# Second block of a two-block transformer kernel: convolution taps spread from attention into retention and short convolution, weight sums issued after the second fold, and one product of an output pair issued early

## The reference, cut to what matters

```python
def conformer_conv(glu_in, w, bias, ln_w, ln_b):
    a, g = jnp.split(glu_in, 2, axis=-1)
    u = depthwise_conv(a * jax.nn.sigmoid(g), w) + bias      # 31 taps
    return jax.nn.silu(layer_norm(u, ln_w, ln_b)).astype(glu_in.dtype)
...
def mixer_output(p, ret_o, att_o, ...):
    r = (head_group_norm(ret_o, ret_gn_w) * jax.nn.silu(p['ret_z'])).astype(dt)
    s = short_conv(p['sc_b'], p['sc_c'], p['sc_x'], sc_conv_w) * jax.nn.silu(p['sc_z'])
    f = conformer_conv(p['cf_glu'], cf_conv_w, ...) * jax.nn.silu(p['cf_z'])
    a = att_o * jax.nn.silu(p['att_z'])
    merged = sum(jax.nn.sigmoid(g) * (br @ w_branch[i])
                 for i, (g, br) in enumerate(zip(gates, (r, s, f, a))))
    return merged @ w_out
...
for l in range(DEPTH):                                       # DEPTH = 2
    px = split_proj(modulate_2(rmsnorm_2(x, norm_w[l]), shift_x, scale_x) @ w_in[l])
    ...                                                      # retention and windowed attention
    x = x + gate_x[:, None] * mixer_output(px, ret_x, att_x, ...)
```

## Time and profile before

| | us |
|---|---|
| median of 3 runs | 3319.2 |
| lowest and highest | 3311.17, 3322.95 |
| profiled execution, its own time | 3317.98 |
| its span | 3316.2 |
| PE busy in the span | 3163.6 |
| DVE busy | 1798.5 |
| ACT busy | 882.0 |

### The profile page before, as it was taken

How to read it: one execution, slowest core, us unless ns; L and a number is a source line. 1 busy time by engine, 2 the same in 40 slices (tenths; PEclk the granted TensorE clock), 3 DMA queues, 4 the chain that set the end, 5 groups by cost and what they waited for, 6 DMA issues and landing times.

```text
span 3316.2 us, 38135 instructions
## 1 busy us (share of the span) xinstructions
PE 3163.6 (95%) x13916; PEld 2101.8 (63%) x13916; DVE 1798.5 (54%) x3620; ACT 882.0 (27%) x1820; POOL 352.4 (11%) x302
## 2 busy tenths in 40 slices
PE   7988998999999999999999999999999999999998
PEld 4743653678853655666665555555557677778887
DVE  2253324788732335886557454444458855754555
ACT  2241221334421222154222221111122622222222
POOL 1300430343300340000120000000000012000000
PEclk9989899999999999999999999999999999999999
DMA  8637786633338796201111112222223011223232
GB/s 271 215 121 251 283 346 204 187 107 102 89 111 270 277 360 195 64 26 45 39 38 51 54 55 57 58 58 57 58 58 83 26 51 51 77 70 89 83 89 64
DMA packets 427399, 397.25 MB, mean 120 GB/s; under 512 B 28080, under 2 KB 362416, under 8 KB 420048
## 3 DMA queue, kind: packets, MB, share of 16 engines
q1 hardware_dynamic: 393520, 352.60, 33.7%
q10 hardware_dynamic: 15264, 22.24, 2.1%
q0 software_dynamic: 18432, 19.98, 1.8%
HBM read 443.54 MB, written 31.92 MB: 143 GB/s over the span
## 4 chain that ended last, share of the span: by engine, by line
PE 60%; DVE 6%; DMA 2%; issue 2%; ACT 2%; ACTq 0%; DVEq 0%
PE psum L768 43%; PE psum L1297 3%; PE psum L994 3%; DVE arena L2315 2%; DMA ring<-in_w_branch 1%; PE psum L1013 1%; PE psum L753 1%; PE psum L1381 1%; PE psum L1421 1%; DVE arena L2312 1%; ACT scratch L1708 1%; PE psum L979 1%; DVE ring L2312 1%; PE psum L1411 1%; PE psum L861 0%
## 5 line engine op out<-in xcount | busy, mean ns | idle before, releaser
L768 PE MATMUL psum<-arena,ring 128*128 128x256 f32 (+1 forms) x2976 | 843.4, 434 | 19.9 <-DVE arena L2312 11.2
L768 PEld LDWEIGHTS psum<-arena,ring 128*128 128x128 f32 x2976 | 562.5, 190 | 269.7 <-DVE arena L2312 15.2
L768 PE MATMUL psum<-hT,ring 128*128 128x256 f32 (+1 forms) x2464 | 696.9, 436 | 0.0
L768 PEld LDWEIGHTS psum<-hT,ring 128*128 128x128 f32 x2464 | 468.2, 190 | 199.5 <-issue 3.2
L1716 ACT ACTIVATE scratch<-psum 128x256 f32<-128x256 f32 (+1 forms) x447 | 190.8, 427 | 1018.3 <-PE psum L768 860.9
L2312 DVE TENSOR_TENSOR psum<-psum,scratch 128x256 f32<-128x256 f32 (+1 forms) x352 | 167.6, 480 | 379.6 <-PE psum L768 273.2
L2312 DVE TENSOR_TENSOR ring<-ring 128x512 f32<-128x512 f32 (+1 forms) x384 | 257.2, 689 | 184.3 <-PE psum L768 172.2
L1716 ACT ACTIVATE arena<-psum 128x512 f32<-128x512 f32 (+5 forms) x426 | 197.3, 497 | 426.8 <-PE psum L768 128.8
L1708 ACT ACTIVATE arena<-psum,cols 128x256 f32<-128x256 f32 (+2 forms) x291 | 134.1, 485 | 498.0 <-PE psum L994 226.5
L2315 DVE SCALAR_TENSOR_TENSOR arena<-arena,vec 128x783 f32<-128x783 f32 (+1 forms) x256 | 228.8, 894 | 9.1
L2315 DVE SCALAR_TENSOR_TENSOR arena<-arena,psum 128x256 f32<-128x256 f32 (+2 forms) x247 | 99.2, 435 | 198.6 <-ACT arena L1708 198.5
(11 more groups left out here) (290 smaller groups left out, 3751.8 us busy)
## 6 DMA issues: line engine op xcount, KB each, us to landing
ring<-in_w_in SPq DMA_DIRECT2D x177, 512.0 KB, 4.2
arena<-in_moe_w SPq DMA_DIRECT2D x44, 1536.0 KB, 10.9
ring<-in_ada_w SPq DMA_DIRECT2D x96, 512.0 KB, 6.0
ring<-in_w_mod SPq DMA_DIRECT2D x48, 512.0 KB, 5.8
ring<-in_ssm_w_in SPq DMA_DIRECT2D x48, 512.0 KB, 5.5
ring<-in_w_branch SPq DMA_DIRECT2D x64, 256.0 KB, 3.1
hT<-in_moe_w SPq DMA_DIRECT2D x10, 1536.0 KB
ring<-in_moe_w SPq DMA_DIRECT2D x10, 1024.0 KB, 5.9
```

What stands on the lines that cost most here:

```text
L768: mm = nc.tensor.matmul(flat(bank_, nb), lhs[:, k, :], rhs(k), start=(start and k == 0), stop=(k == kd_ - 1), skip_group_check=True)
```

## The change

Four things change, all in the second block.

1. In layer 1 (`cx` false) the taps are dealt out anew: 32 in the first pairs (chunk 0 exactly), 2 in each of rounds 0 to 5 (12), and 84 in pairs 1 to 13: 7 in pair 1, 4 in pairs 2, 4, 6 and 8, 8 in pairs 3, 5, 7 and 9 to 12, and 5 in pair 13. Up to three of a pair's taps are its `late` part, between C22 and C12. The total stays 128. Chunk 1 now outlives attention, so layer 1's buffer for it is put into `cT`, and the wait of the gate part for chunk 1's convolution falls away in layer 1.
2. In every `combine` that has a `mid` and a next pair, in both layers, `w_sums` stands behind C22 instead of ahead of it.
3. In pairs 2h + 2 the `mid` taps stand ahead of `ret_states`, in both layers.
4. In `pair` for pair 50, in both layers, PE takes the weights and a bank of pair 51 and issues pair 51's P1 between P5 of pair 50 and the wait for `mrg` chunks 4 to 7. Pair 51 then starts with its P2. The seven products of each pair stay the same.

```diff
--- before.py
+++ after.py
@@ -485,7 +485,8 @@
...
         mQ = Arena(at=late_at)
-        cu = [cu_first, br_free[:, 4 * CW - 813:4 * CW], mQ.take(813), mQ.take(813)]
+        cu = [[cu_first, br_free[:, 4 * CW - 813:4 * CW], mQ.take(813), mQ.take(813)]]
+        cu.append([cu_first, cT.rearrange("p k n -> p (k n)")[:, 0:813]] + cu[0][2:4])
         pT_window = arena[:, k_raw_at:k_raw_at + 3 * S].rearrange("p (a b) -> p a b", b=S)
@@ -611,8 +612,8 @@
...
-            row = cu[c][:, 15:15 + S].rearrange("p (b h n) -> p h b n", h=2, n=P)[:, h]
-            return [(row, 0, 2)] + ([(cu[c][:, 15 + CO + P * h:15 + CO + P * h + P].unsqueeze(1), 2, 3)] if ctx_here("cf_g", l, c) else [])
+            row = cu[l][c][:, 15:15 + S].rearrange("p (b h n) -> p h b n", h=2, n=P)[:, h]
+            return [(row, 0, 2)] + ([(cu[l][c][:, 15 + CO + P * h:15 + CO + P * h + P].unsqueeze(1), 2, 3)] if ctx_here("cf_g", l, c) else [])
@@ -757,11 +758,17 @@
...
-            def pair(a, b, src, ready=None, between=None):
+            ahead = {}
+
+            def pair(a, b, src, ready=None, between=None, then=None):
...
                 nb = blocks(a)
-                wa, used_a = take(a)
-                wb, used_b = take(b)
+                begun = ahead.pop(a, None)
+                if begun is None:
+                    wa, used_a = take(a)
+                    wb, used_b = take(b)
+                else:
+                    (wa, used_a), (wb, used_b), (x, x_full) = begun
@@ -775,16 +782,21 @@
...
                 s = lambda j: sum_tile(a)[:, kd_ * j:kd_ * j + kd_, :]
-                x, x_full = job(*b, "0")
+                if begun is None:
+                    x, x_full = job(*b, "0")
                 if ready == "m":
...
                         eng.wait_ge(vector_done, pe.at(("mrg", a[1], c)))
-                product(x, wa[:, 0:kd_, :], low(0), True, ("P1", a))
+                if begun is None:
+                    product(x, wa[:, 0:kd_, :], low(0), True, ("P1", a))
                 if ready == "m":
...
                     product(z, s(0), total(0), True, ("P5", a))
+                    a_, b_ = then
+                    ahead[a_] = take(a_), take(b_), job(*b_, "0")
+                    product(ahead[a_][2][0], ahead[a_][0][0][:, 0:kd_, :], low(0), True, ("P1", a_))
                     for c in range(4, 8):
@@ -1542,7 +1554,7 @@
...
                     for j in range(4):
-                        pair(*todo[50 + j], mrg, ready="m" if j == 0 else None)
+                        pair(*todo[50 + j], mrg, ready="m" if j == 0 else None, then=todo[51] if j == 0 else None)
                 if upto > 7:
@@ -2117,7 +2129,7 @@
...
                         eng.wait_ge(tensor_done, ac.at(("full",) + j))
-                        act(cu[0][:, 15 + CO:15 + CO + L], bank(j)[:, 0:L], ACT.Tanh, scale=0.5).then_inc(scalar_done, ac.step([("free",) + j, ("cf_t", 0, 0, "c")]))
+                        act(cu[0][0][:, 15 + CO:15 + CO + L], bank(j)[:, 0:L], ACT.Tanh, scale=0.5).then_inc(scalar_done, ac.step([("free",) + j, ("cf_t", 0, 0, "c")]))
                     for i, (one, two) in enumerate(first_pairs(l)):
@@ -2141,7 +2153,7 @@
...
                             eng.wait_ge(tensor_done, ac.at(("full",) + j))
-                            if (c, tag) == (3, "x0"):
+                            if (l, c, tag) == (0, 3, "x0"):
                                 eng.wait_ge(vector_done, ac.at(("cf_conv", l, 1)))
@@ -2366,7 +2378,7 @@
...
                     mid()
-                if nxt:
+                elif nxt:
                     w_sums(*nxt)
@@ -2374,6 +2386,8 @@
...
                     [("C22", a), ("full",) + jb1 if dst_b is None else name_b + ("1",)]))
+                if mid and nxt:
+                    w_sums(*nxt)
                 if late:
@@ -3044,7 +3058,7 @@
...
                         for o in (0, 15 + S) + ((15 + CO + L,) if cx else ()):
-                            v.memset(cu[c][:, o:o + 15], 0.0).then_inc(vector_done, ve.step([("cu_free", l, c)]))
+                            v.memset(cu[l][c][:, o:o + 15], 0.0).then_inc(vector_done, ve.step([("cu_free", l, c)]))
                     if cx:
@@ -3063,9 +3077,9 @@
...
                             if k == 0:
-                                ts(acc, cu[c][:, 0:w_], cw(0, c)).then_inc(vector_done, ve.step())
+                                ts(acc, cu[l][c][:, 0:w_], cw(0, c)).then_inc(vector_done, ve.step())
                             elif k < 31:
-                                stt(acc, cu[c][:, k:k + w_], cw(k, c), acc, ALU.mult, ALU.add).then_inc(vector_done, ve.step())
+                                stt(acc, cu[l][c][:, k:k + w_], cw(k, c), acc, ALU.mult, ALU.add).then_inc(vector_done, ve.step())
                             else:
@@ -3100,22 +3114,22 @@
...
                         b, free = full("cf_a", 0, 0, "c")
-                        u = cu[0][:, 15 + CO:15 + CO + L]
+                        u = cu[0][0][:, 15 + CO:15 + CO + L]
                         stt(u, u, 1.0, b[:, 0:L], ALU.add, ALU.mult).then_inc(vector_done, ve.step(free))
...
                     combine(*first[1], mid=lambda: taps(3))
-                    taps(4 if cx else 7)
+                    taps(4 if cx else 6)
                     combine(*first[2], mid=lambda: taps(6 if cx else 3), late=lambda: (rotate_q(0), rotate_q(1)))
...
                     combine(*first[3], mid=lambda: taps(3))
-                    taps(4 if cx else 7)
+                    taps(4 if cx else 6)
                     combine(*first[4], mid=lambda: taps(6 if cx else 3), late=lambda: (rotate_q(2), rotate_q(3)))
...
                     taps(3 if cx else 1)
-                    combine(*first[5], mid=lambda: taps(6 if cx else 5), late=lambda: taps(3))
+                    combine(*first[5], mid=lambda: taps(6 if cx else 3), late=lambda: taps(3 if cx else 0))
                     glu(3)
@@ -3165,8 +3179,8 @@
...
                         att_norm(r, n, j)
-                        if tap[0] < 64:
-                            taps(min(64 - tap[0], 3 if cx else 5))
+                        if tap[0] < 64 if cx else r < 6:
+                            taps(min(64 - tap[0], 3) if cx else 2)
                         if r % 3 == 2 if cx else r % 2:
@@ -3287,24 +3301,24 @@
...
                     key_scale()
-                    combine(*todo[1], mid=lambda: taps(5))
+                    combine(*todo[1], mid=lambda: taps(5), late=lambda: taps(0 if cx else 2))
                     for h in range(3):
...
                             ret_norm(h - 1, zi[h - 1])
-                        combine(*todo[2 * h + 2], mid=lambda: (ret_states(h), taps(3)))
+                        combine(*todo[2 * h + 2], mid=lambda: (taps(3), ret_states(h)), late=lambda: taps(0 if cx else 1))
                         zi.append(z_mul("ret_z", l, h + 1, cx, h + 1, -0.5))
-                        combine(*todo[2 * h + 3], mid=lambda: taps(6))
+                        combine(*todo[2 * h + 3], mid=lambda: taps(6 if cx else 5), late=lambda: taps(0 if cx else 3))
                         ret_center(h)
...
                     ret_norm(2, zi[2])
-                    combine(*todo[8], mid=lambda: (ret_states(3), taps(3)))
+                    combine(*todo[8], mid=lambda: (taps(3), ret_states(3)), late=lambda: taps(0 if cx else 1))
                     v.memset(sc_u[:, :, :], 0.0).then_inc(vector_done, ve.step())
                     sc_conv(0)
-                    combine(*todo[9], mid=lambda: taps(6))
+                    combine(*todo[9], mid=lambda: taps(6 if cx else 5), late=lambda: taps(0 if cx else 3))
                     ret_center(3)
@@ -3318,9 +3332,10 @@
...
                     for c in (1, 2, 3):
-                        combine(*todo[8 + 2 * c], mid=(lambda: taps(6)) if c < 3 else None)
+                        combine(*todo[8 + 2 * c], mid=(lambda: taps(6 if cx else 5)) if c < 3 else None, late=(lambda: taps(0 if cx else 3)) if c < 3 else None)
                         sc_conv(c)
-                        combine(*todo[9 + 2 * c], mid=(lambda: taps(min(6, 128 - tap[0]))) if c < 3 else cf_center)
+                        combine(*todo[9 + 2 * c], mid=(lambda: taps(min(6 if cx else 5, 128 - tap[0]))) if c < 3 else cf_center,
+                                late=(lambda: taps(min(0 if cx else 3, 128 - tap[0]))) if c < 3 else None)
                         sc_out(c, sc_z(c))
```

## The result

| | before | after |
|---|---|---|
| median of the runs, us (12 each) | 3318.4 | 3300.5 |
| lowest and highest | 3311.17, 3327.77 | 3295.71, 3310.82 |
| profiled execution, its own time and span | 3317.98, 3316.2 | 3296.91, 3295.1 |
| PE, DVE, ACT busy | 3163.6, 1798.5, 882.0 | 3153.5, 1791.4, 881.4 |

The ratio of the times is 0.995, with a 95% interval of 0.994 to 0.996. The kernel became 18 us faster, where 16 were forecast (3303, within 3296 to 3312).

What follows compares the result with a forecast made beforehand. PE was taken as the bound, busy 3163.6 of 3316.2 us, so only its waits could pay. Terms 7.4 + 3.1 + 2.9 - 3.2 + 4.3 + 1.7 = 16.2 gave 3301.8, stated as 3303; range 3296 to 3312.

Steps and rivals of the forecast that it cites:

- Attention, 7.4 forecast: Layer 1's attention: fewer taps a round shorten PE's waits, gaining 7.4 us, between 5.0 and 8.0.
- The first wait: Ahead of round 0's turn in layer 1's attention: PE's 4.9 us wait shrinks by 2.3 to 2.6.
- The half clock: Round 0's turn in attention: a shorter wait may spare PE's spell at 1.2 GHz, worth 1.25 us.
- the later waits: Later attention rounds: two waits of 2.5 us together and one of 1.7 go, 4.2; 3.8 counted.
- The rival in which ACT and banks hold attention: Layer 1's attention: turns wait for copies, only 2.3 of 7.4 us comes, 3308; chance 0.12.
- Weight sums in layer 0's retention, 3.1 forecast: Last products of pairs 3, 5 and 7: three waits for C22 go, 3.1 us, or 2.0 if held.
- Short convolution, 2.9 net forecast: Layer 1's short convolution: four waits for C22, 3.3 us, go; net 2.9 after pair 9's delay, between 1.5 and 3.3.
- The charge of 0.4 at `ret_center(3)`: Pair 9 of layer 1: `ret_center(3)` waits for three late taps and `w_sums`, ending its chain about 0.4 us later.
- Late taps in layer 1's retention, -3.2 forecast: Heads 0 to 2: `w_sums` stretched beside POOL by 1.07 us each delays PE, losing 3.2, between 0.1 and 3.9.
- One product ahead, 4.3 and 1.7 forecast: Pair 50: pair 51's P1 fills PE's wait, gaining 4.3 us in layer 0 (at least 2.6) and 1.7 in layer 1.
- At nothing: Fewer taps in first pairs, taps ahead of `ret_states` and earlier C22 at pair 18: counted as no gain or loss.
- the half clock that I had kept as a lower bound: Pair 19: longer idle time could halve PE's clock once, 1.3 us lost, counted only in the lower bound.

Runs made afterwards that it cites:

- e5: Changed kernel with weight sums back ahead of C22 in layer 1's pairs 3, 5, 7 and 9; layer 1's retention 2.5 us shorter, median not given.
- the four moves: Changed kernel with sums ahead of C22 in rotations, pairs 3, 5, 7, 9 and pair 18, and round 0's taps behind `att_max(1)`; median 3291.3 us.
- e3: Kernel before the change with only the weight sums moved behind C22; layer 0's retention gains 3.9 us, median not given.
- e6: Changed kernel with POOL scaling only two of four query tiles in layer 1's retention, computation incomplete; median of six runs 3302.56 us.
- e2: Changed kernel with the weight sums ahead of C22 again; median 3300.8 us.
- e4: Changed kernel with weight sums ahead of C22 again in the first pairs with rotations; stretch through layer 1's attention 2.6 us shorter, median not given.

## Why the prediction was right, and where its terms were off

The sum was 16.2. From layer 0's retention on, the trace gained 16.0 (15.5 with layer 0's first pairs and attention); the median gained 17.9. That is closer than the terms were.

**Attention, 7.4 forecast.** The dealing alone gives 9.2 to 10.2 in part D (against the two executions with the old dealing). The first wait shrank by 2.6 rather than 2.3. The kernel with five taps in round 0 gives 2.36 for three taps. The other 0.3 is that the first of round 0's taps is now the first of chunk 1, a `tensor_scalar` of 0.49, where each of the five before was one of 0.78. The half clock went as forecast, 1.5 by start times, but in part by luck: behind the same 2.30 it fell in one of six executions (e5). All 4.2 of the later waits went, and each wait also takes the overlap of its neighbours with it, 0.2 to 0.3, which no row of waits shows. The rival in which ACT and banks hold attention did not come with two taps a round; at the first turn ACT did become the last to be waited for with the four moves, once round 0's queue on DVE was 1.6 shorter still.

**Weight sums in layer 0's retention, 3.1 forecast, 3.9 measured** (A, twice). The waits shown were three, 3.1; the 0.8 above it is 0.27 for each, the same overlap.

**Short convolution, 2.9 net forecast.** The four waits went, as forecast; with the overlaps they were worth 4.4 (E and F of e3). Their cause was half right: the sums' place alone clears them, and five taps in place of six, which alone clear 2.2 of 3.3, add nothing beside it. The charge of 0.4 at `ret_center(3)` was 1.0, and 1.6 more for a half clock that no term held.

**Late taps in layer 1's retention, -3.2 forecast, -1.5 measured.** The step that failed is the size: I took the excess of the earlier trace rows, 1.07, on each head in full, and named waits of about 1.4 a head, where 0.82 came. In the changed kernel the sums overlap only the second of POOL's instructions and take 2.71, an excess of 0.69, and the idle time ahead of `ret_center` swallowed 0.2 of it. The prices fit each other: 1.77 us of idle time without late taps (e3), less 2.33 of taps, leaves `ret_center` 0.56 late; 0.50 was measured; with sums at 2.01 (e6) nothing is left. The Trainium skill, "GPSIMD Engine Reference", section on its key points, has contention between GpSimd and VectorE for instructions with two SBUF inputs. The runs agree: with POOL's work cut, the same three operations fall from 2.71 to 2.01. But contention is not yet a cost: in e5 the taps are stretched too (2.76), and PE lost nothing by it, since the queue had room behind them.

**One product ahead, 4.3 and 1.7 forecast.** In layer 0 part C gives 4.3 (the product alone). In layer 1 the wait fell by 1.9; e2, without a half clock at pair 19, shows 2.1 in G.

**At nothing: two edits were not nothing.** The prediction said that PE never waits in the first pairs, and looked only at taps there. The new place of `w_sums` bears on these pairs as well, ahead of C12 and so of ACT's tanh and the copy behind it: 1.5 by the waits, 2.1 by start times. At pair 18 the waits of 1.21 and 2.12 became one of 3.59, which by start times costs 0.1 at most, and the half clock that I had kept as a lower bound came, 1.6. The losses outside the sum are then 2.1 in rotations, 0.1 and 1.6 at pair 19, 0.6 and 1.6 at head 3: 6.0. The gains above their terms are 1.8 in attention, 0.8 in layer 0's retention, 1.1 in short convolution, 1.7 in layer 1's retention and 0.2 to 0.4 at layer 1's pair 50: 5.7, and the clock behind the norm between the layers adds 0.2. The sum was right because these cancelled, and that is luck.

## What to carry to other kernels

Work that is moved behind a milestone in one queue delays all that waits for the next milestone: list for every call of a shared helper who waits for the last thing it makes, here C12 and `ret_center`, and not only for the one it was moved for. One rule for all calls was worth nothing in sum; exceptions to it in the rotations and in layer 1's retention, with round 0's taps moved, were worth 7.7 us by the traces and 9 by the medians. When the queue ahead of a wait is shortened, look at once which other engine's work ends just ahead of it, since the gain stops there (of 1.6 in round 0 only 0.9 came, of 2.12 at pair 19 only 1.3). And where executions differ by 10 us ahead of the changed code, compare start times of the same instructions behind it: those parts repeat to 0.1 us but for the granted clock, which moved them by 1.4 to 2.4 behind a wait and by up to 1.2 around the norm. Start times also show what sums of waits hide: at pair 19 waits of 1.21 and 2.12 delay PE as much, within 0.1 us, as one of 3.59.

## What the runs showed of the hardware

The half clock behind a wait is no fixed function of the wait's length. Over the twelve profiled executions, with the same matmuls behind the same wait, in layer 1: after 1.63 at head 3 it fell in none of 8; after 2.30 at attention's first turn in 1 of 6; after 1.21 and 2.12 at pair 19 in 2 of 5; after 2.53 at pair 50 in 2 of 3; after 2.61 at head 3 in 3 of 4; after 3.59 at pair 19 in 5 of 6; after 4.66 and 4.93 in 4 of 4. In layer 0: after 1.45 at attention's second turn, with 0.20 right behind it, in 3 of 12; after 1.83 at pair 16 in none of 12; after 1.93 at head 3 in 4 of 12; after 2.22 at pair 19 in 1 of 7; after 2.30 at the fourth turn in 4 of 9; after 2.76 at pair 50 in 3 of 3. The shortest of them, in e4 (timeline of PE; the eight matmuls of 1.76 take 1.14 in e5):

```profile
1430.19 0.63 PE L1423 MATMUL psum<-const,arena 128*128 128x128 f32 x4 [1.45 <-DVE arena L2320]
...
1431.65 1.76 PE L1407 MATMUL psum<-arena 64*128 64x256 f32 x8
```

Where the half clock fell behind waits of up to 3.59, it made the work behind them 1.4 to 2.3 us longer. After the 1.45 it cost nothing, since the fourth turn then waited 0.66 in place of 2.30. So an idle time of even 1.5 to 2 us can be followed by it, those of 1.5 to 4 are to be priced with a chance, and the longest seen here with the whole of it.

POOL's part is mutual. Its two query scalings take 3.00 (e5) or 2.99 (before) where the weight sums take 3.09 beside them, and 2.50 where only the second of them meets the sums, which then take 2.71 (after); apart from it (e6) the sums take 2.01. Three taps ran 2.76 instead of 2.33 beside the same work.
